# A down projection from seven block products, with its input rows stored by token tile, partition and parity

## Chip, cores, metric

One core of one Trainium2 chip runs the whole program in one launch. The metric is the device time in microseconds; the kernel before has a median of 3306.24 us of 3 runs (3305.8 to 3311.68).

## What is computed

The reference is one decoder block over 16 meta tokens and 2048 tokens of width 1024: two mixing branches (RWKV-7 and S5), their gated sum times `w_out`, and a gated MLP with a causal convolution over tokens. What the change touches most is its end:

```
up = hn @ ffn_w_up                                    # (2064, 1024) @ (1024, 5632)
a  = causal_dwconv(up[..., :2816], conv_w, conv_b)
f  = (gelu_tanh(a) * up[..., 2816:]) @ ffn_w_down     # (2064, 2816) @ (2816, 1024)
h  = h + rms_norm(f, norm_ffn_post)
```

The meta tokens are dropped from the output. All data are float32. Each matrix product is made of three TensorE products: every operand is split into a rounded high part (`_hi`, written by ScalarE as a copy to float32r) and the rest (`_lo`, written by VectorE as raw minus high), and hi*hi, hi*lo and lo*hi are added in PSUM.

## The kernel before

The program is a row of stages, each ended by a barrier of all engines (`stage_ends`): the input projection with the S5 branch, the RWKV chunks (`rwkv_chunks`), the branch mix with the output projection (`branch_mix`, `token_projection` with the name mixout), the up projection (`ffn_up`), and the down projection (`token_projection`, name down). Each engine works through its own list in order and waits on semaphores; nearly all DMAs are issued by SP, in SP's order.

**Down stage.** Two passes over the 22 blocks of 128 hidden channels, 11 blocks (`k_tiles`) in each. In a pass the weights of 11 blocks x 1024 columns are split once, and then 16 token tiles of 128 tokens follow. For each tile, SP loads the hidden values (`load_acts`, 11 blocks x 128 tokens, in runs of 512 bytes since `hidden` is `[22, 128, 2048]` in DRAM), ScalarE makes `a_hi` (L2549), VectorE `a_lo` (L2613), and TensorE runs 11 k x 2 column halves x 3 matmuls (L2516). After pass 0 ScalarE copies PSUM to `sums` (L2555); after pass 1 VectorE adds PSUM to `sums` (L2622), ScalarE squares and takes the root (L2565, L2567), VectorE scales (L2631) and adds the residual rows (L2636), and SP stores the row. The weights of the stage are loaded by L2431 into several spare places; the first is loaded in the up stage (L2840), as is the first input tile (L2843).

**Up stage.** It works already with seven block products in place of eight. It goes over 11 pairs of hidden blocks, first for tokens 0 to 1023 (FIRST), then for 1024 to 2047 (SECOND). In a pair each of 14 parts (q) has its high and low weight made seven parts ahead (L2910, L3030); differences of weights are made by VectorE (L3025). The convolution (L3081, L3083), gelu (L2948) and the gating multiply (`gated`, L3093) follow a half row at a time, and SP stores the half row (L2819). The last half row's gating comes after the last matmul, just before the barrier.

**End of the chunk stage.** Groups of two chunks of 64 tokens are taken one after the other. Behind each group comes a tail: flat copy (L1932), affine on ScalarE (L1938), add and multiply with loaded rows on GpSimd (L2040, L2042), high part on ScalarE (L1942), low part on GpSimd (L2044). SP asks for the mix stage's first weight, activations and gate before that (L1492), and loads the last group's bonus and gate rows (L1433) when the group before it is scaled. The mix stage begins with the split of its first weight (L2223 on ScalarE, L2265 on VectorE), and TensorE's first product there (L2186) waits for it.

## Time and profile before

| | |
|---|---|
| median of 3 runs | 3306.24 us |
| the profiled execution | 3308.43 us, its span 3306.6 us |
| TensorE busy | 3140.9 us, 95% of the span, 25690 matmuls |
| VectorE, ScalarE, GpSimd busy | 1846.0, 1292.4, 120.6 us |
| mean granted TensorE clock | 0.981 |
| last matmuls of the up stage | about 2803 us |
| matmuls of the down stage | 2112, from 2815.7 to 3297.2 us |

All rows below are from this one execution. Times are us from the start of the span unless marked ns. PE is TensorE's matmuls, PEld its weight loads (they run beside the matmuls), DVE is VectorE, ACT is ScalarE, POOL is GpSimd, SPq are SyncE's DMA issues. A line number such as L2516 is that of the kernel above. The granted clock is a share of full speed, 1.00 being 2.4 GHz and 0.50 being 1.2 GHz.

### The profile page before, as it was taken

The page shows a single profiled execution, that of the slowest core. Times are in us where ns is not written, and L with a number is a line of the kernel's source. Part 1 is how long each engine was busy: PE and PEld are TensorE (multiplying, and loading weights), DVE is VectorE, ACT ScalarE, POOL GpSimd, SP SyncE. Part 2 cuts the span into 40 slices and gives each one's busy share as a digit, 9 for nine tenths or more (in the row PEclk, how much of TensorE's full clock was granted, in tenths as well). Part 3 has the DMA queues.
Part 4 walks back from the last instruction along what each step waited for, and adds up shares of the span by engine and source line. Part 5 has one row for each costly group of instructions (what it writes and reads, how often), then busy time and mean ns, then how long its engine had stood idle before and what let it go on. Part 6 is the DMA issues. An engine that isn't in the chain of part 4 may idle for free. (4 is left out here: it accounts for less than half of the span.)

```text
span 3306.6 us, 69209 instructions
## 1 busy us (share of the span) xinstructions
PE 3140.9 (95%) x25690; PEld 2802.9 (85%) x25690; DVE 1846.0 (56%) x3531; ACT 1292.4 (39%) x2265; POOL 120.6 (4%) x126
## 2 busy tenths in 40 slices
PE   8999999999978888879999979999999999999998
PEld 7999989999967777769998869999888887788887
DVE  7666655555545666553344476666766665212333
ACT  6211136767753444441123344444544443312211
POOL 0000000000001222200000000000000000000000
PEclk9999999999988999989999989999999999999999
DMA  5333346656543334333346613333522222412342
GB/s 159 112 138 123 118 156 203 194 188 197 188 122 81 92 92 95 107 121 119 121 160 205 209 57 113 111 102 102 166 83 76 76 82 68 158 51 74 120 125 90
DMA packets 391252, 409.57 MB, mean 124 GB/s; under 512 B 140352, under 2 KB 332736, under 8 KB 387184
## 3 DMA queue, kind: packets, MB, share of 16 engines
q1 hardware_dynamic: 390096, 408.20, 39.5%
q8 instruction: 60, 0.98, 0.1%
q14 instruction: 40, 0.33, 0.0%
q10 hardware_dynamic: 1056, 0.07, 0.0%
HBM read 260.58 MB, written 147.59 MB: 123 GB/s over the span
## 5 line engine op out<-in xcount | busy, mean ns | idle before, releaser
L2889 PE MATMUL psum<-up_x,up_w_hi 128*128 128x512 f32 (+2 forms) x1540 | 353.0, 351 | 12.5 <-ACT up_w_hi L2910 6.9
L2895 PE MATMUL psum<-up_x,up_w_hi 128*128 128x512 f32 (+2 forms) x1540 | 352.8, 351 | 0.8 <-DVE up_x L3047 0.8
L2892 PE MATMUL psum<-up_x,up_w_lo 128*128 128x512 f32 (+2 forms) x1540 | 351.6, 350 | 0.0
L2889 PEld LDWEIGHTS psum<-up_x,up_w_hi 128*128 128x128 f32 x1540 | 260.0, 190 | 54.1 <-issue 7.0
L2895 PEld LDWEIGHTS psum<-up_x,up_w_hi 128*128 128x128 f32 x1540 | 260.0, 190 | 41.3 <-DVE up_x L3047 1.1
L2892 PEld LDWEIGHTS psum<-up_x,up_w_lo 128*128 128x128 f32 x1540 | 260.0, 190 | 40.6
L2516 PE MATMUL psum<-down_w_hi,down_a_hi 128*128 128x512 f32 x704 | 275.0, 391 | 12.3 <-DVE down_w_lo L2675 12.3
L2516 PE MATMUL psum<-down_w_lo,down_a_hi 128*128 128x512 f32 x704 | 274.8, 390 | 0.0
L2516 PE MATMUL psum<-down_w_hi,down_a_lo 128*128 128x512 f32 x704 | 274.8, 390 | 0.0
L694 PE MATMUL psum<-x_hi,proj_w_hi 128*128 128x416 f32 (+1 forms) x640 | 245.5, 384 | 0.0
L577 PE MATMUL psum<-x_hi,proj_w_hi 128*128 128x416 f32 (+1 forms) x640 | 224.7, 351 | 0.0
L694 PE MATMUL psum<-x_lo,proj_w_hi 128*128 128x416 f32 (+1 forms) x640 | 223.8, 350 | 0.0
L577 PE MATMUL psum<-x_hi,proj_w_lo 128*128 128x416 f32 (+1 forms) x640 | 223.4, 349 | 0.0
L577 PE MATMUL psum<-x_lo,proj_w_hi 128*128 128x416 f32 (+1 forms) x640 | 223.4, 349 | 0.0
L694 PE MATMUL psum<-x_hi,proj_w_lo 128*128 128x416 f32 (+1 forms) x640 | 223.3, 349 | 0.0
L3030 DVE TENSOR_TENSOR up_w_lo<-up_weight,up_w_hi 128x512 fp32r<-128x512 f32 x176 | 118.9, 686 | 107.1 <-ACT up_w_hi L2910 107.1
L2516 PEld LDWEIGHTS psum<-down_w_hi,down_a_hi 128*128 128x128 f32 x704 | 132.8, 189 | 40.4 <-issue 12.7
L2613 DVE TENSOR_TENSOR down_a_lo<-down_a_raw,down_a_hi 128x1408 fp32r<-128x1408 f32 x32 | 51.9, 1622 | 196.8 <-ACT down_a_hi L2549 192.8
L2516 PEld LDWEIGHTS psum<-down_w_hi,down_a_lo 128*128 128x128 f32 x704 | 132.7, 188 | 27.7
L2516 PEld LDWEIGHTS psum<-down_w_lo,down_a_hi 128*128 128x128 f32 x704 | 132.7, 189 | 27.6
L2910 ACT ACTIVATE up_w_hi<-up_weight 128x512 fp32r<-128x512 f32 x176 | 109.6, 624 | 85.4 <-PE psum L2895 76.6
L811 ACT ACTIVATE proj_pre<-psum 128x416 f32<-128x416 f32 (+1 forms) x70 | 36.1, 517 | 258.6 <-PE psum L577 203.2
...
## 6 DMA issues: line engine op xcount, KB each, us to landing
...
chunk_pre<-scratch_roles SPq DMA_DIRECT2D x128, 128.0 KB, 2.7
```

What stands on the lines that cost most here:

```text
L577: mm = nc.tensor.matmul(psum[:, PRODUCT_BANKS[n], 0:WIDTHS[n]], w[:, v, k, :], x[:, k, block_of(n)], start=(k == 0 and w is w_hi and x is ...
L694: mm = nc.tensor.matmul(psum[:, GATE_BANKS[n], 0:WIDTHS[n]], w[:, v, k, :], x[:, k, block_of(n)], start=(k == 0 and w is w_hi and x is x_h ...
L811: nc.scalar.activation(pre[:, 2 + STARTS[n]:2 + STARTS[n] + WIDTHS[n]], done, ACT.Copy).then_inc(evacuated, 1)
L2516: mm = nc.tensor.matmul(psum[0:n, 2 * u + h, :], a[:, u, k, 0:n], w[:, k, h * HALF:(h + 1) * HALF], start=(k == 0 and a is a_hi and w is w ...
L2613: nc.vector.tensor_tensor(a_lo[:, u, :, 0:n], (a_raw if n == P else a_meta)[:, :, 0:n], a_hi[:, u, :, 0:n].bitcast(F32), ALU.subtract).the ...
L2889: nc.tensor.matmul(out, w_hi[:, q % 7, k, :], x_hi(phase, step)[:, k, cols], start=opens and k == 0, stop=False, skip_group_check=True)
L2892: nc.tensor.matmul(out, w_lo[:, q % 7, k, :], x_hi(phase, step)[:, k, cols], start=False, stop=False, skip_group_check=True)
L2895: mm = nc.tensor.matmul(out, w_hi[:, q % 7, k, :], x_lo(phase, step)[:, k, cols], start=False, stop=closes and k == K4 - 1, skip_group_che ...
L2910: nc.scalar.activation(w_hi[:, q % 7], weight_of(part, step), ACT.Copy).then_inc(w_hi_ready, 1)
L3030: V.tensor_tensor(w_lo[:, q % 7], weight_of(part, step), w_hi[:, q % 7].bitcast(F32), ALU.subtract).then_inc(w_lo_ready, 1)
```

## The change

The down projection becomes a function of its own, `ffn_down`. Tokens are halved (tile t and tile 8 + t), hidden blocks are halved by parity (block 2k and 2k + 1), output columns are halved (512 and 512). Of the 2 x 2 x 2 block products seven are made, of sums and differences of the quarters, in the order P_2, P_5, P_3, P_1, P_6, P_7, P_4: each of 8 tiles x 11 k x 3 matmuls of 128x512, with one PSUM bank for each tile. The quarters of the result are gathered in `sums`: ScalarE copies them out after P_2, P_5 and P_3, VectorE adds PSUM to them after P_1, P_6 and P_7. The rows of tokens 0 to 1023 are finished after P_6, the others after P_4 straight from PSUM.

The inputs: `hidden` lies in DRAM as `[token tile, partition, parity, 1 + 11, 128]`, with one block of each row unused, so that a tile's input is one run of 5632 bytes per partition; the up stage stores each half row in runs of 512 bytes. In its SECOND phase the up stage also makes the sums S1 = A21 + A22 and S2 = S1 - A11 for each pair (`sum_rows`, two 128x1024 operations on VectorE), loads the A11 row for them and stores both (`hidden_sums`). Two further differences (for P_3 and P_7) are made tile by tile in `ffn_down` (`act_sum`), from two loaded inputs. Weights are handled in items of 128x512, one to four of them in a tile, one product ahead, in a ring of 18; four products need the difference of two loaded weights (`weight_sum`), and two of these differences are stored to DRAM (`w_down_sums`) and loaded again.

At the end of the chunk stage, the last two groups' tail is moved from GpSimd to VectorE, the last group's in two halves by lane; its bonus and gate rows are loaded earlier into `pre`; and the first mix weight is split there (`next_split`) and no longer at the start of the mix stage. For this some buffers get fixed places (`CHUNK_SPACE`).

The diff, cut to its core:

```diff
-    hidden = dram("hidden", [M_FF, P, SEQ])
+    hidden = dram("hidden", [SEQ // P, P, 2, 1 + M_FF // 2, P])
+    hidden_sums = dram("hidden_sums", [2, SEQ // P // 2, P, M_FF // 2, P])
+    w_down_sums = dram("w_down_sums", [2, M_FF // 2, P, D_MODEL // 2])
...
-            for g in (GROUPS - 2, GROUPS - 1):
-                sp.wait_ge(scaled, g)
-                load_post(g)
+            sp.wait_ge(scaled, GROUPS - 2)
+            load_post(GROUPS - 2)
+            sp.wait_ge(toks_done[1], GROUPS)
+            for q_, src in enumerate((gate_dram, bonus_dram)):
+                for lane in BOTH:
+                    at_t = T - WIDE + lane * S
+                    sp.dma_start(pre[:, q_, lane], src[:, :, at_t:at_t + S].rearrange("j p t -> p j t")).then_inc(last_post_loaded, 16)
...
+                    raw, hi, lo, _, hi_made, lo_made = next_split
+                    for n_, part in enumerate((slice(0, 1), slice(1, 3))):
+                        dve.wait_ge(hi_made, n_ + 1)
+                        V.tensor_tensor(lo[:, part], raw[:, part], hi[:, part].bitcast(F32), ALU.subtract).then_inc(lo_made, 1)
                     state(a, 1)
                     for c in (b - 2, a, b):
                         norm_mean(c)
                         norm_squares(c)
                         norm_divide(c)
+                    before = g * WIDE - WIDE
+                    gained(g - 1, 0, flat[:, 1], post[:, 1], post[:, 0], post_loaded, 32 * g)
+                    low_part(g - 1, 0, flat[:, 1], before, WIDE)
+                    for lane in BOTH:
+                        gained(g, lane, flat[:, 0, :, lane * S:(lane + 1) * S], pre[:, 1, lane], pre[:, 0, lane], last_post_loaded, 64)
+                    for lane in BOTH:
+                        low_part(g, lane, flat[:, 0, :, lane * S:(lane + 1) * S], g * WIDE + lane * S, S)
...
+                    raw, hi, _, loaded, hi_made, _ = next_split
+                    act.wait_ge(loaded, 16)
+                    for part in (slice(0, 1), slice(1, 3)):
+                        A.activation(hi[:, part], raw[:, part], ACT.Copy).then_inc(hi_made, 1)
...
-                cols = slice(phase * 2 * UP_COLS, (phase + 1) * 2 * UP_COLS)
-                sp.dma_start(hidden_out[bass.ds(2 * m + half, 1), :, cols].rearrange("m p t -> p (m t)"), hidden[:, half]).then_inc(done, 16)
+                n = 2 * UP_COLS // P
+                sp.dma_start(hidden_out[phase * n:(phase + 1) * n, :, half, bass.ds(m + 1, 1), :].rearrange("t p o c -> p t (o c)"),
+                             hidden[:, half].rearrange("p (t c) -> p t c", c=P)).then_inc(done, 16)
+            def load_row(m):
+                for n in range(2):
+                    sp.wait_ge(rows_stored[n], 16 * m + 16)
+                sp.wait_ge(stored[0], 16 * FF_PAIRS + 16)
+                sp.dma_start(held_a.rearrange("p (t c) -> p t c", c=P),
+                             hidden_out[0:2 * UP_COLS // P, :, 0, bass.ds(m + 1, 1), :].rearrange("t p o c -> p t (o c)")).then_inc(row_loaded, 16)
+            def store_rows(m, done):
+                sp.wait_ge(rows_summed, 2 * m + 2)
+                for n, total in enumerate((held_b, held_a)):
+                    sp.dma_start(hidden_sums[n, :, :, bass.ds(m, 1), :].rearrange("t p o c -> p t (o c)"), total.rearrange("p (t c) -> p t c", c=P)).then_inc(done[n], 16)
...
+                if phase == SECOND and not first:
+                    store_rows(m - 1, rows_stored)
+                if phase == SECOND:
+                    load_row(m)
+                if final:
+                    sp.wait_ge(stored[1], 16 * FF_PAIRS + 16)
+                    sp.wait_ge(product_done[P_1], units_before(SECOND, FF_PAIRS))
+                    sp.wait_ge(product_done[P_2], units_before(SECOND, FF_PAIRS))
+                    sp.dma_start(down_first, down_first_source).then_inc(down_first_loaded, 16)
+                    sp.dma_start(down_w_first, down_w_source).then_inc(down_w_loaded, 16)
...
+            def sum_rows(m, g):
+                dve.wait_ge(b_used[0], g + 2)
+                dve.wait_ge(b_used[1], g + 2)
+                dve.wait_ge(rows_stored[0], 16 * m + 16)
+                V.tensor_tensor(held_b, hidden[:, 0], hidden[:, 1], ALU.add).then_inc(rows_summed, 1)
+                dve.wait_ge(row_loaded, 16 * m + 16)
+                dve.wait_ge(rows_summed, 2 * m + 1)
+                V.tensor_tensor(held_a, held_b, held_a, ALU.subtract).then_inc(rows_summed, 1)
...
+                        if phase == SECOND and not first:
+                            sum_rows(m - 1, g - 1)
...
+            sum_rows(LAST, 2 * FF_PAIRS - 1)
...
+DOWN_RAW, DOWN_W_RAW, DOWN_RING = 4, 4, 18
...
+        ACTS_OF = {P_2: (A12,), P_5: (S1,), P_3: (A12, S2), P_1: (A11,), P_6: (S2,), P_7: (A11, A21), P_4: (A22,)}
...
+        WEIGHTS_OF = {P_2: (B21,), P_5: (B12, B11), P_3: (B22,), P_1: (B11,), P_6: (B22, T1), P_7: (B22, B12), P_4: (B21, T2)}
...
+        def items_in(q):
+            s, t = step_of(q) + 1, tile_of(q)
+            if s == STEPS:
+                return []
+            return [(s, k) for k in range(K_PAIRS) if min(k, TILES - 1) == t]
...
+            def load_act(q, n):
+                j = act_loads.index((q, n))
+                if j >= DOWN_RAW:
+                    sp.wait_ge(acts_lo, act_loads[j - DOWN_RAW][0] + 1)
+                which, t = ACTS_OF[step_of(q)][n], tile_of(q)
+                if which in (S1, S2):
+                    src = act_sums[which - S1, t]
+                else:
+                    src = acts[t + (TILES if which in (A21, A22) else 0), :, 1 if which in (A12, A22) else 0, 1:]
+                sp.dma_start(raw(q, n), src).then_inc(raw_loaded[raw_slot[q, n]], 16)
...
+            def load_weight(s, k):
+                for n, which in enumerate(WEIGHTS_OF[s]):
+                    before = w_loads[w_loads.index((s, k, n)) - DOWN_W_RAW]
+                    sp.wait_ge(w_lo_done, number_of[before[:2]] + 1)
+                    if before[:2] in kept:
+                        kept_stored(before[:2])
+                    if which in (T1, T2):
+                        kept_stored((P_5 if which == T1 else P_6, k))
+                    sp.dma_start(held_w_raw[:, w_slot[s, k, n]], weight_source(which, k)).then_inc(w_raw_loaded[w_slot[s, k, n]], 16)
...
+            def store_kept(s, k):
+                j = kept.index((s, k))
+                sp.wait_ge(w_summed, w_sum_count[s, k])
+                if j >= 2:
+                    kept_stored(kept[j - 2])
+                sp.dma_start(w_sums[0 if s == P_5 else 1, k], held_w_raw[:, w_slot[s, k, 0]]).then_inc(t_stored[j % 2], 16)
...
+            for k in range(DOWN_W_RAW, K_PAIRS):
+                sp.dma_start(weight_raw(0, k), weight_source(B21, k)).then_inc(staged_loaded[k], 16)
+            load_act(1, 0)
+            load_weight(1, 0)
+            load_weight(1, 1)
+            sp.dma_start(gains, gain).then_inc(gain_loaded, 16)
+            for q in range(LAST + 1):
+                if step_of(q) == P_2 and tile_of(q) == TILES - 2:
+                    sp.wait_ge(late_stored, 48)
+                for n in range(len(ACTS_OF[step_of(q + 2)]) if q + 2 <= LAST else 0):
+                    load_act(q + 2, n)
+                for s, k in items_in(q):
+                    if (s, k) in kept:
+                        store_kept(s, k)
+                    if number_of[s, k] + 2 < len(items):
+                        load_weight(*items[number_of[s, k] + 2])
+                if row_of(q) is not None:
+                    load_rows(row_of(q))
+                if q >= 2 and row_of(q - 2) is not None:
+                    store_row(row_of(q - 2))
...
+                opens, closes = s in (P_2, P_5, P_1), s in (P_2, P_3, P_4)
+                if 1 <= s <= 3:
+                    pe.wait_ge(copied, q - TILES + 1)
+                elif s > 3:
+                    pe.wait_ge(added, q - TILES + 1 - 3 * TILES)
+                pe.wait_ge(acts_hi, q + 1)
+                pe.wait_ge(acts_lo, q + 1)
+                for k in range(K_PAIRS):
+                    if t == 0:
+                        pe.wait_ge(w_lo_done, number_of[s, k] + 1)
+                    product(t, q, k, a_hi, w_hi, opens and k == 0, False)
+                    product(t, q, k, a_hi, w_lo, False, False)
+                    mm = product(t, q, k, a_lo, w_hi, False, closes and k == K_PAIRS - 1)
+                    if t == TILES - 1 and k < K_PAIRS - 1:
+                        mm.then_inc(weight_used, 1)
+                mm.then_inc(tile_done, 1)
...
+            high(0)
+            for k in range(6):
+                weight_high(0, k)
+            high(1)
+            for k in range(6, K_PAIRS):
+                weight_high(0, k)
+            nc.scalar.preload_act_table(ACT.Sqrt)
+            act.wait_ge(eps_ready, 1)
+            for q in range(LAST + 1):
+                s = step_of(q)
+                if 1 <= q < LAST:
+                    high(q + 1)
+                if q and step_of(q - 1) in (P_2, P_5, P_3):
+                    copy(q - 1)
+                if s == P_4:
+                    square_known(q)
+                if q and step_of(q - 1) == P_4:
+                    square_second_half(q - 1)
+                for item in items_in(q):
+                    weight_high(*item)
+                if q and step_of(q - 1) == P_6:
+                    square_first_half(q - 1)
+            square_second_half(LAST)
...
+            low(0)
+            for k in range(6):
+                weight_low(0, k)
+            low(1)
+            for k in range(6, K_PAIRS):
+                weight_low(0, k)
+            for q in range(LAST + 1):
+                s = step_of(q)
+                if q and step_of(q - 1) in (P_1, P_6, P_7):
+                    add(q - 1)
+                due = items_in(q)
+                for item in due[:2]:
+                    weight_sum(*item)
+                if 1 <= q < LAST:
+                    low(q + 1)
+                for item in due[:2]:
+                    weight_low(*item)
+                for item in due[2:]:
+                    weight_sum(*item)
+                for item in due[2:]:
+                    weight_low(*item)
+                if q + 2 <= LAST:
+                    act_sum(q + 2)
+                if s == P_4:
+                    if q == TILES * P_4:
+                        dve.wait_ge(gain_loaded, 16)
+                    gain_known(q)
+                if q and step_of(q - 1) == P_6:
+                    if q - 1 == TILES * P_6:
+                        dve.wait_ge(gain_loaded, 16)
+                    finish_first_half(q - 1)
+                if q and step_of(q - 1) == P_4:
+                    finish_second_half(q - 1)
+            finish_second_half(LAST)
```

## Rows read from the trace of the kernel before

**Rows 1.** The chain of waits, in order of time: start, duration, what.

```profile
2815.74 481.47 PE psum L2516 x2112
...
3301.51 1.23 DVE down_sums L2636
```

**Rows 2.** Busy time by stretch; the first row names the columns.

```profile
core 0: us, PE busy (x) PEld busy (x) DVE busy (x) ACT busy (x) POOL busy (x), PEclk, DMA share, GB/s
2600.00:2700.00 100.00, 100.00 (x435) 81.28 (x434) 69.50 (x100) 43.08 (x65) 0.00 (x0) 1.00 0.24 84
2816.00:2818.00 2.00, 2.00 (x5) 1.52 (x5) 1.88 (x2) 1.06 (x1) 0.00 (x0) 0.50 1.02 406
2822.00:2824.00 2.00, 2.00 (x11) 1.65 (x10) 1.94 (x2) 1.72 (x2) 0.00 (x0) 1.00 1.04 418
2860.00:2960.00 100.00, 100.00 (x443) 82.79 (x442) 11.38 (x7) 16.06 (x14) 0.00 (x0) 1.00 0.17 46
```

**Rows 3.** Groups of instructions, 2400 to 3307: busy us, mean ns, idle before.

```profile
L3030 DVE TENSOR_TENSOR up_w_lo<-up_weight,up_w_hi 128x512 fp32r<-128x512 f32 x80 | 54.1, 687 | 50.0 <-ACT up_w_hi L2910 50.0
...
L2613 DVE TENSOR_TENSOR down_a_lo<-down_a_raw,down_a_hi 128x1408 fp32r<-128x1408 f32 x32 | 51.9, 1622 | 196.8 <-ACT down_a_hi L2549 192.8 <-DMA down_gains<-in_ffn_post 4.0
L2910 ACT ACTIVATE up_w_hi<-up_weight 128x512 fp32r<-128x512 f32 x79 | 49.3, 624 | 37.9 <-PE psum L2895 37.9
L2549 ACT ACTIVATE down_a_hi<-down_a_raw 128x1408 fp32r<-128x1408 f32 x32 | 44.0, 1376 | 10.6 <-DMA down_a_raw<-scratch_hidden 6.6 <-PEq L2506 3.3
...
L3067 DVE TENSOR_TENSOR up_a_pre<-psum,up_a_pre 128x512 f32<-128x512 f32 x32 | 22.0, 689 | 12.4 <-PE psum L2895 11.7
...
L2631 DVE SCALAR_TENSOR_TENSOR down_sums<-down_sums,down_stat,down_gains 128x1024 f32 (+1 forms) x16 | 20.6, 1285 | 0.6
L2636 DVE TENSOR_TENSOR down_sums<-down_sums,down_rows 128x1024 f32 (+1 forms) x16 | 19.6, 1226 | 1.3
```

**Rows 4.** DMA queue, 2811 to 2832: packets, MB, share of 16 engines.

```profile
q1 hardware_dynamic: 3334, 7.68, 97.7%
```

**Rows 5.** The DMA queue from 2860 to 2960.

```profile
q1 hardware_dynamic: 9119, 4.62, 16.9%
```

**Rows 6.** The DMA queue from 2748 to 2751.5.

```profile
q1 hardware_dynamic: 288, 0.52, 43.8%
```

**Rows 7.** Timeline from up to down stage: start, duration, engine, instruction, [idle before].

```profile
2808.11 1.23 DVE L3093 TENSOR_TENSOR up_hidden<-up_hidden,up_b_pre 128x1024 f32<-128x1024 f32 x1 [1.12 <-ACT up_hidden L2948]
2811.24 0.06 DVE L2599 MEMSET down_eps<- 128x1 f32 x1 [1.91 <-PEq L3192]
2811.29 0.81 SPq L2431 DMA_DIRECT2D down_w_raw<-in_w_down  x2
...
2812.15 4.04 SPq L2431 DMA_DIRECT2D down_sums<-in_w_down  x8
...
2814.37 1.22 DVE L2675 TENSOR_TENSOR down_w_lo<-down_first_raw,down_w_hi 128x1024 fp32r<-128x1024 f32 x1
...
2815.74 0.76 PE L2516 MATMUL psum<-down_w_hi,down_a_hi 128*128 128x512 f32 x1 [12.26 <-DVE down_w_lo L2675]
```

**Rows 8.** Timeline at the end of the chunk stage.

```profile
1395.47 0.50 SPq L1492 DMA_DIRECT2D mix_weight<-in_w_mix_tiles  x1
...
1407.91 0.38 ACT L1914 ACTIVATE chunk_u<-psum 128x256 f32<-128x256 f32 x1 [5.69 <-PE psum L1530]
...
1409.71 0.42 DVE L1804 TENSOR_TENSOR chunk_m<-chunk_m,psum 128x256 f32<-128x256 f32 x1 [9.19 <-PE psum L1530]
...
1422.49 1.36 DVE L1828 TENSOR_TENSOR chunk_y_unit<-chunk_y,chunk_stat 128x256 f32<-128x256 f32 x1
...
1430.88 1.26 POOL L2044 TENSOR_TENSOR rwkv_y_lo<-chunk_flat,rwkv_y_hi 128x512 fp32r<-128x512 f32 x1 [0.74 <-ACT rwkv_y_hi L1942]
...
1435.41 0.71 PE L2186 MATMUL psum<-rwkv_y_hi,mix_w_hi 128*128 128x416 f32 x1 [10.81 <-ACT mix_w_hi L2223]
```

**Rows 9.** Timeline at the end of the kernel.

```profile
3302.76 0.35 SPq L2423 DMA_DIRECT2D out_h<-down_sums  x1
```

292 lines of the change are left out of this document (254 added, 38 removed).

## The prediction

> **What bounds the kernel now.** I read the chain of waits first. It shows one piece of 481.47 us from 2815.74 on, the 2112 matmuls of L2516 in the down projection, and after it only the few us of the last row [rows 1]. So in this stage TensorE's own work is the time. The stretches say the same: from 2860 to 2960 TensorE is busy all of the time, VectorE 11%, ScalarE 16%, DMA 17%, and the granted clock is 1.00, its level of 2.4 GHz [rows 2]. The pace there is 443 matmuls in 100 us, 0.2257 us each. Over the whole piece it is 481.47 / 2112 = 0.228: at 2816 the clock is at 0.50 (1.2 GHz) after an idle stretch, and at 2822 it is back at 1.00 [rows 2]. The second half of the up stage is bound in the same way, with VectorE at 70% [rows 2].
>
> **Matmuls removed.** Before: 16 token tiles x 22 k blocks x 2 column halves x 3 = 2112. After: 7 block products x 8 tiles x 11 k x 3 = 1848, each of the same shape, three in a row into one bank as before. 264 x 0.2257 = 59.6 us less. (By 0.228 it is 60.2.)
>
> **What the other engines must do beside them.** A tile of a product is now 33 matmuls, 33 x 0.2257 = 7.45 us, where one pass over a tile took twice that. In each, ScalarE makes a_hi (1.38) and 11/8 weight parts (0.62 each); VectorE makes a_lo (1.62) and as many w_lo (0.69) [rows 3]. Added are: the difference of two weights (0.69, as a 128x512 subtract), in tiles of P_3 and P_7 the difference of two inputs (about 1.62, by the a_lo row, same shape), the addition to C out of PSUM (0.69), and for each row of P_6 a scale (1.29) and an add (1.23) [rows 3]. The worst ordinary tile is one of P_6: 0.69 + 0.69 + 1.62 + 0.69 + 0.16 + 1.29 + 1.23 = 6.4 us of 7.45. It fits, if loads are there. The last tile of a product has four weight items instead of one, 3 x 1.38 = 4.1 us more. For the change from P_6 to P_7 this meets the row's 2.7 and the input difference of 1.62: 12.1 us of VectorE in one tile, and in the next again 8.0.
>
> **The stall I expect.** A weight is loaded only two items ahead, so in such a last tile the load of item 9 goes out when w_lo of item 7 is done, some 5 us into the tile, and two loads of 256 KB need 1.5 us of queue (below) and some 2 us of latency. VectorE stands near 3 us there. Then it is at about 16.6 us when it begins the next tile's work, and has a_lo for the tile after ready 3 us later, at 19.6, where TensorE wants it at 14.9: 4.7 us, and 0.5 to 1 in the tile after. I take 5.5 us (bounds 0 and 10). At the other product changes there is neither row nor input difference: VectorE is through at about 11.7, a_lo follows at 14.0 to 14.7, just in time: 0 taken, up to 3 each. A stall may bring the clock down once: the row at 2816 shows the half level after an idle stretch, and the 13 or so matmuls up to 2822 cost about 2.5 us more than at 0.2257. I take 1.5 for this.
>
> **DMA.** The bytes go up from 23 MB of inputs and 11.5 MB of weights to 72 x 0.72 = 52 MB, 121 x 0.262 = 31.7 MB of weights and 5.8 MB of weight differences stored; with rows and results 106 MB in 430 us, 247 GB/s. What the 16 engines do when busy depends on the piece. With nearly all in 4 KB pieces they moved 7.68 MB in 97.7% of 21 us, 374 GB/s [rows 4]; in 512-byte pieces 4.62 MB in 16.9% of 100 us, 273 GB/s [rows 5]; in 2 KB pieces 0.52 MB in 43.8% of 3.5 us, 340 GB/s [rows 6]. The new layout is what makes this bearable: an input tile is read in pieces of 5.6 KB instead of 512 bytes, so 52 MB take 139 us at 374 GB/s and not 190. The worst tiles are those of P_6: 0.72 + 0.72 + 0.52 + 0.52 = 2.5 MB in 7.45 us, 334 GB/s, some 90% of the engines' time. In its last tile it is 1.44 + 2.1 + 1.05 = 4.6 MB, 12 to 13 us of work; the inputs were asked for two tiles ahead, which is why I count this into the 5.5 and not beside it.
> In the Trainium skill, "DMA: Bandwidth & Descriptors", section Specifications, the limit of HBM for one core is put at about 358 GB/s. By that P_6 would run at 93% of the limit and its last tile would take 12.9 us. The trace disagrees on the level: 406 and 418 GB/s in 2 us stretches [rows 2].
>
> **Beginning of the down stage.** The first weight is 512 wide instead of 1024: w_lo takes 0.69 and not 1.22 [rows 3, 7], so TensorE starts 0.5 us sooner. But on ScalarE the split of the second input tile now stands between weights 5 and 6, and its load is behind seven weight loads: these are 1.83 MB and it is 0.72, 6.8 us at 374 GB/s and 2 of latency, 8.8 after the start of the stage. a_hi, w_hi, and on VectorE a_lo and w_lo follow by about 12.3. TensorE, started 3.8 after it and at half clock for some 5 us, wants weight 6 at 10.3. Stall 1.8 us (0 to 4).
>
> **End of the up stage.** It ends with the gating multiply of the last half row (2808.11, 1.23), the barrier, and TensorE's next matmul at 2815.74 [rows 7]. Behind that multiply stand now two sums of 128x1024, 2 x 1.22 by the same row, and two stores that SP can issue only then, 0.4 to 0.5 each by the issues in [rows 7]. Nothing hides them: +3.0 us (2.4 to 4). In the ten pairs before, the same sums (2.4 us of some 38) lie in VectorE's free 30%. The stores in 512-byte pieces and one row load are 2.6 MB, 9.7 us of DMA at 273 GB/s in a pair of 38 us with 24% used. SP holds the sums' stores and waits for them before it fetches a row; the next weights behind them come to land some 5 us before VectorE wants them. Cost 0; up to 1 us per pair if that order bites.
>
> **Chunk stage to mix stage.** Now the last group is finished on GpSimd in three steps of 1.26 one after another with ScalarE between, ending at 1432.14; the mix weights are split after the barrier, and TensorE's wait there is 10.81 [rows 8]. After: the weight split moves to the start of the last group, where ScalarE was idle 5.7 us and VectorE 9.2, and the weight had been asked for at 1395.47 [rows 8]. The tail runs on VectorE in 0.42 to 0.69 steps: previous group added, multiplied (1424.4), high part 1425.1; flat copy and affine of lane 1 on ScalarE until 1426.7; lane 1 add and multiply 1427.6; high 1428.05; two lows, 1428.5. That is 3.6 us sooner; from the end of that work to TensorE it was 3.27, of which about 1.5 were the two splits. 3.6 + 1.5 = 5.1 us saved (3 to 6.5).
>
> **End of the kernel.** After the last matmul (2815.74 + 481.47 = 3297.2) before: add, square, root, reciprocal, scale and add until 3302.74, then the store [rows 1, 9]. After: square of 512 out of PSUM 0.6, gain 0.69, reciprocal 0.17, two halves of 0.66, less than 3 us with handoffs. With the same store behind it: -3.0.
>
> **Sum.** -59.6 + 5.5 + 1.5 - 0.5 + 1.8 + 3.0 - 5.1 - 3.0 = -56.4 us. The profiled execution before took 3308.43 (span 3306.6), so 3252.0; it lay 2.2 above the median of 3306.24, so I predict 3250.
>
> **Rivals.**
> 1. *The weight loads bind at every product change.* If at the other five the round trip (load, difference, high, low) shows too, at 4 us each and with some clock loss: +22, 3272. For it: two items ahead is little, and [rows 6] shows 340 GB/s at best for these pieces. Against: the 7.45 us of slack of the tile after.
> 2. *No stall at all.* If VectorE's backlog is taken up by the two tiles of inputs held: 3250 - 8.8 = 3241. Against: 12.1 + 8.0 us of work stand on VectorE in two tiles of 7.45.
> 3. *The up stage pays.* The sums stand in VectorE's queue ahead of the next pair's weight sums and low parts. At 1 us of TensorE per pair over 11 pairs: 3261. Against: VectorE's free 30%, and low parts made seven steps ahead.
> 4. *Slower: SP's single queue makes each tile a round trip.* All loads, stores and their waits stand in SP's order; the input load of tile q+2 is behind a weight load that waits for w_lo of this tile. If a pair of weights then lands only 5 us after it is asked for and VectorE stands for it in each tile, a tile of P_7 is 5.3 + 5 = 10.3 us, 2.9 too long. The products before a double-weight product have 32 such tiles: 93 us, 3343. It decides from a mean tile of 8.5 us on (56 x 1.05 = 59 us). For it: one queue, and VectorE waiting in order. Against: the load is for the item two further, one whole tile ahead.
> 5. *The change doesn't do what it says* is not left: the loops give 1848.
>
> **Chances.** Forecast 0.55 (own range 3243 to 3260); rival 1 0.17; rival 2 0.12; rival 3 0.08; rival 4 0.08. Between rival 4's full price and the others lies little, so slower by over 0.2% (6.6 us, about what can be told from no change here) gets 0.08, within it 0.02, faster 0.90. Range 3238 to 3280: rival 2 below with the bounds of the start and the tail, rival 1 above.
>
> **What would show it.** L2516's heirs number 1848 at 0.226 us, from first to last about 430 us, with one wait of 4 to 6 us on a_lo or a difference at the start of P_7, and one near 2 us in the first tile. TensorE's wait after the up stage grows from 12.3 to about 15; at the mix stage it falls from 10.8 to 5 or 6. The second half of the up stage keeps 435 matmuls per 100 us. Wrong it is if VectorE waits for weight DMAs in most tiles, if the down stage lasts over 450 us, or if the up stage loses its pace.

## The result, and the profile after

The changed kernel takes 3288.47 us (median of 5 runs, the fastest 3284.51), the kernel before 3309.95 (5 runs). The ratio is 0.9933, with a 95% interval of 0.9919 to 0.9947: 22 us faster, where 56 were forecast, and outside the range of 3238 to 3280. Two of the five runs, at 3500.89 and 13375.18 us, are far off all others and are left out of the ratio. The profiled execution took 3288.47 (span 3286.6, mean clock 0.975).

The chain of waits of the changed kernel shows at once what is different. Where [rows 1] had one piece of 481.47 us there are three pieces of matmuls, and between them weight stores, weight loads and input loads (start, duration, what):

```profile
2841.80 5.05 DMA scratch_w_down_sums<-down_w_raw
2848.28 6.62 DMA scratch_w_down_sums<-down_w_raw
2856.34 6.42 DMA scratch_w_down_sums<-down_w_raw
2864.19 6.50 DMA scratch_w_down_sums<-down_w_raw
2872.12 6.68 DMA scratch_w_down_sums<-down_w_raw
...
2898.94 166.20 PE psum L3402 x726
3066.48 5.75 DMA scratch_w_down_sums<-down_w_raw
3073.19 4.07 DMA scratch_w_down_sums<-down_w_raw
3077.76 3.52 DMA down_w_raw<-scratch_w_down_sums
...
3089.41 31.78 PE psum L3402 x132
...
3127.22 10.33 DMA down_raw<-scratch_hidden
...
3157.27 9.60 DMA down_raw<-scratch_hidden
...
3227.74 52.64 PE psum L3402 x231
```

The stretches, against [rows 2]. The up stage keeps its 435 matmuls in 100 us. 2860 to 2960 holds the border from P_2 to P_5: 413 matmuls and not 443, with a clock of 0.97. The last row is P_6 from its second to its seventh tile:

```profile
core 0: us, PE busy (x) PEld busy (x) DVE busy (x) ACT busy (x) POOL busy (x), PEclk, DMA share, GB/s
2600.00:2700.00 100.00, 100.00 (x435) 81.32 (x434) 74.12 (x102) 43.24 (x66) 0.00 (x0) 1.00 0.38 116
2860.00:2960.00 100.00, 96.45 (x413) 78.85 (x412) 38.86 (x40) 32.07 (x42) 0.00 (x0) 0.97 0.60 201
3090.00:3135.00 45.00, 45.00 (x194) 37.15 (x193) 33.75 (x39) 19.53 (x30) 0.00 (x0) 0.97 0.92 313
```

The timeline from the up to the down stage, against [rows 7], and at the end of the first tile (idle time before an instruction in brackets):

```profile
2805.93 1.22 DVE L3161 TENSOR_TENSOR up_hidden<-up_hidden,up_b_pre 128x1024 f32<-128x1024 f32 x1 [1.12 <-ACT up_hidden L3016]
2807.24 1.23 DVE L3168 TENSOR_TENSOR down_first_raw<-up_hidden 128x1024 f32<-128x1024 f32 x1
2808.57 1.23 DVE L3171 TENSOR_TENSOR down_a_raw<-down_first_raw,down_a_raw 128x1024 f32<-128x1024 f32 x1
...
2812.33 3.97 SPq L3374 DMA_DIRECT2D down_sums<-in_w_down  x7
...
2816.13 1.19 PE L3402 MATMUL psum<-down_w_parts,down_a_hi 128*128 128x512 f32 x2 [14.83 <-DVE down_w_parts L3538]
...
2816.65 0.33 SPq L3335 DMA_DIRECT2D down_raw<-scratch_hidden  x1
...
2823.79 1.38 ACT L3434 ACTIVATE down_a_hi<-down_raw 128x1408 fp32r<-128x1408 f32 x1 [5.92 <-DMA down_raw<-scratch_hidden]
...
2827.48 1.22 PE L3402 MATMUL psum<-down_w_parts,down_a_hi 128*128 128x512 f32 x2 [5.25 <-DVE down_w_parts L3538]
```

TensorE's wait at the mix stage, which was 10.81 [rows 8], and what follows the last matmul of the kernel, where the add of 1.23 stood at 3301.51 [rows 1]:

```profile
1429.09 0.71 PE L2231 MATMUL psum<-rwkv_y_hi,mix_w_hi 128*128 128x416 f32 x1 [6.88 <-DVEq L2301]
...
3279.98 0.39 PE L3402 MATMUL psum<-down_w_parts,down_a_lo 128*128 128x512 f32 x1
3280.41 0.60 ACT L3463 ACTIVATE down_squares<-psum 128x512 bf16<-128x512 f32 x1 [6.41 <-PE psum L3402]
...
3281.95 1.42 DVE L3578 SCALAR_TENSOR_TENSOR down_sums<-down_sums,down_stat,down_rows 128x512 f32<-128x512 f32 x2
3282.73 0.99 SPq L3396 DMA_DIRECT2D out_h<-down_sums  x2
```

**A measure for the rest.** An undisturbed tile of 33 matmuls takes 7.48 us from start to start in this trace, and 44 of the 56 tiles take just that. What a tile takes beyond it I call its loss. In all it is 45.1 us: 10.2 in the first tile, 6.7 at P_2 to P_5, 11.2 at P_1 to P_6, 15.9 at P_6 to P_7, 1.2 at P_7 to P_4. P_3, P_1 and the insides of the products lose nothing. 28 us of it are waits of TensorE. The other 17 are the rest, put down to matmuls at half clock, which the records show at the stage's start and in the stretches that follow the waits. The longest wait at P_1 to P_6 and the longest at P_6 to P_7:

```profile
3082.72 1.22 PE L3402 MATMUL psum<-down_w_parts,down_a_hi 128*128 128x512 f32 x2 [4.00 <-DVE down_w_parts L3538]
...
3161.89 1.19 PE L3402 MATMUL psum<-down_w_parts,down_a_hi 128*128 128x512 f32 x2 [5.10 <-DVE down_a_lo L3518]
```

**What happens at P_1 to P_6.** The timeline of SyncE and VectorE in the last tile of P_1:

```profile
3065.25 0.42 SPq L3335 DMA_DIRECT2D down_raw<-scratch_hidden_sums  x1
3065.76 0.69 DVE L3534 TENSOR_TENSOR down_w_raw<-down_w_raw 128x512 f32<-128x512 f32 x1
3066.48 0.33 SPq L3362 DMA_DIRECT2D scratch_w_down_sums<-down_w_raw  x1
...
3072.30 0.33 SPq L3351 DMA_DIRECT2D down_w_raw<-in_w_down  x1
3072.73 0.37 SPq L3351 DMA_DIRECT2D down_w_raw<-scratch_w_down_sums  x1
3073.19 0.38 SPq L3362 DMA_DIRECT2D scratch_w_down_sums<-down_w_raw  x1
...
3077.32 0.33 SPq L3351 DMA_DIRECT2D down_w_raw<-in_w_down  x1
...
3081.37 0.69 DVE L3534 TENSOR_TENSOR down_w_raw<-down_w_raw 128x512 f32<-128x512 f32 x1 [3.94 <-DMA down_w_raw<-scratch_w_down_sums]
```

Item 7's difference is stored at 3066.48, behind an input of 704 KB, and lands 5.75 later (the chain). Only then may its place be loaded again (3072.30), and only after that does SP come to item 8's store (3073.19), though its difference was ready at 3069.3. This lands 4.07 later, and the next load goes out at 3077.32. So the landing of item 7's store (5.75), that of item 8's (4.07) and the load of item 10 (3.52, from 3077.76) stand one after another: 14.9 us from 3066.48 to the subtraction at 3081.37, while TensorE has one tile of 7.48 us for four items. SP's own waits, 2815 to 3290 (total us, times, longest), show how much of its time goes there:

```profile
SPq L3351 <- DVE down_w_parts L3538: 129.8, 38, 10.7
SPq L3355 <- DMA scratch_w_down_sums<-down_w_raw: 99.8, 22, 6.3
SPq L3335 <- DVE down_a_lo L3518: 55.2, 9, 7.1
```

### The profile page after: what moved, and what is told of

Read it like the earlier page. It is cut to its first block and busy times, and to the rows that moved or that the text cites. A ratio compares the mean times of both kernels' runs of the same rounds, so it can differ in the third digit from the quotient of the medians.

```text
span 3286.6 us, 69045 instructions
## 1 busy us (share of the span) xinstructions
PE 3098.7 (94%) x25426; PEld 2762.6 (84%) x25426; DVE 1985.2 (60%) x3726; ACT 1342.8 (41%) x2373; POOL 114.7 (3%) x120
## 5 line engine op out<-in xcount | busy, mean ns | idle before, releaser
L3402 PE MATMUL psum<-down_w_parts,down_a_hi 128*128 128x512 f32 x1232 | 391.1, 400 | 43.1 <-DVE down_w_parts L3538 29.6
L3402 PEld LDWEIGHTS psum<-down_w_parts,down_a_hi 128*128 128x128 f32 x1232 | 236.6, 193 | 97.8 <-issue 32.1
L3402 PE MATMUL psum<-down_w_parts,down_a_lo 128*128 128x512 f32 x616 | 244.8, 397 | 0.0
L3434 ACT ACTIVATE down_a_hi<-down_raw 128x1408 fp32r<-128x1408 f32 x56 | 77.3, 1380 | 249.0 <-PE psum L3402 187.6
L3518 DVE TENSOR_TENSOR down_a_lo<-down_raw,down_a_hi 128x1408 fp32r<-128x1408 f32 x56 | 91.0, 1625 | 117.3 <-ACT down_a_hi L3434 117.2
L3402 PEld LDWEIGHTS psum<-down_w_parts,down_a_lo 128*128 128x128 f32 x616 | 119.1, 193 | 25.6
L2976 ACT ACTIVATE up_w_hi<-up_t_sums 128x512 fp32r<-128x512 f32 x132 | 82.9, 630 | 138.8 <-PE psum L2961 129.9
```

Source lines behind the costliest of these rows:

```text
L2976: nc.scalar.activation(w_hi[:, q % 7], weight_of(part, step), ACT.Copy).then_inc(w_hi_ready, 1)
L3402: return nc.tensor.matmul(psum[:, bank, :], a[:, q % SLOTS, k, :], w(step_of(q), k), start=opens, stop=closes, skip_group_check=True)
L3434: nc.scalar.activation(a_hi[:, q % SLOTS], raw(q, 0), ACT.Copy).then_inc(acts_hi, 1)
L3518: V.tensor_tensor(a_lo[:, q % SLOTS], raw(q, 0), a_hi[:, q % SLOTS].bitcast(F32), ALU.subtract).then_inc(acts_lo, 1)
```

## The experiments

"Loss" is that of the profiled execution, in the order: first tile, P_2 to P_5, P_1 to P_6, P_6 to P_7, P_7 to P_4. Ratios are to the kernel before, with their 95% intervals; the differences between experiments are of medians. All but e12_chunk_alone change the kernel after. The same code reached the mix stage between 1426.4 and 1435.3 us in these profiles, and the interval of a ratio reaches some 5 us to either side, so differences of less than that between totals aren't told from nothing; they are read from the losses. Nor does a profiled execution always lie at its run's median: e9's is 8.8 us above it, e8's 5.5 below. A border that an edit doesn't touch varies too, P_2 to P_5 between 6.7 and 10.1 us with SP issuing stores and loads as before (after, e4, e5, e10), P_6 to P_7 between 14.2 and 16.5 (after, e1, e2, e3), the first tile between 8.2 and 10.2 (after, e4, e5, e6, e10).

| run | median us | ratio (95%) | loss |
|---|---|---|---|
| after | 3288.5 | 0.9919 to 0.9947 | 10.2, 6.7, 11.2, 15.9, 1.2 = 45.1 |
| e1_no_kept | 3275.1 | 0.9887 to 0.9920 | 9.7, 0, 4.4, 15.7, 2.3 = 32.1 |
| e2_kept_by_act | 3277.0 | 0.9892 to 0.9925 | 9.9, 2.3, 5.6, 14.2, 2.5 = 34.6 |
| e3_act_first | 3286.8 | 0.9912 to 0.9945 | 3.1, 11.2, 10.5, 16.5, 0.6 = 41.9 |
| e4_no_rows_p6 | 3280.7 | 0.9906 to 0.9948 | 8.2, 7.3, 9.1, 10.5, 0.4 = 35.4 |
| e5_no_finish_p6 | 3283.1 | 0.9909 to 0.9942 | 8.2, 9.1, 10.7, 11.2, 2.4 = 41.7 |
| e6_acts_by_act | 3278.6 | 0.9884 to 0.9917 | 8.4, 7.3, 11.2, 11.7, 1.2 = 39.7 |
| e7_old_layout | 3304.0 | 0.9969 to 0.9992 | 11.2, 7.2, 16.2, 24.2, 1.8 = 60.6 |
| e8_order | 3295.3 | 0.9941 to 0.9974 | 8.9, 6.5, 9.4, 21.7, 2.6 = 49.1 |
| e9_five_raw | 3291.8 | 0.9937 to 0.9970 | 7.9, 13.7, 12.8, 17.0, 0 = 51.4 |
| c4_both_by_act | 3273.4 | 0.9883 to 0.9916 | 8.1, 0, 8.5, 12.7, 0.6 = 29.9 |
| e10_p7_one_input | 3283.6 | 0.9913 to 0.9947 | 8.4, 10.1, 9.0, 8.2, 0.1 = 35.8 |
| c8_five_kept_by_act | 3271.6 | 0.9869 to 0.9902 | 7.8, 2.7, 3.5, 15.8, 0 = 29.8 |
| c5_five_by_act | 3262.9 | 0.9847 to 0.9880 | 7.5, 0, 0.8, 10.9, 0 = 19.2 |
| c6_five_act_first | 3256.9 | 0.9823 to 0.9853 | 2.5, 0, 1.8, 9.0, 0 = 13.3 |
| c7_five_first_order | 3262.1 | 0.9844 to 0.9874 | 2.7, 0.8, 1.0, 13.2, 0.5 = 18.1 |
| c9_rows_later | 3254.2 | 0.9824 to 0.9859 | 2.7, 0, 1.7, 7.0, 0 = 11.4 |

**e1_no_kept and e2_kept_by_act.** The stores of weight differences left out (e1: other weights are loaded in their place), or issued by ScalarE instead of SP (e2).

```diff
                 for s, k in items_in(q):
-                    if (s, k) in kept:
-                        store_kept(s, k)
```
```diff
# e2, in ScalarE's weight_high(s, k), after the copy to w_hi
+                if (s, k) in kept:
+                    nc.scalar.dma_start(w_sums[0 if s == P_5 else 1, k], held_w_raw[:, w_slot[s, k, 0]]).then_inc(t_stored[j % 2], 16)
```


> Leaves out the 22 stores of weight differences to DRAM; where such a difference was loaded again, a piece of w_down is loaded in its place, so the P_6 and P_4 products use other weights. In the changed kernel the tiles at the change from P_2 to P_5 lose 6.7 us over 7.48 us each, those at the change from P_1 to P_6 lose 11.2, those around P_6 to P_7 15.9, the first tile 10.2. Theory A (SP stands for each of these stores, whose landing waits behind a 704 KB input load, before it asks for the next weights): P_5's loss falls from 6.7 to below 1, P_6's from 11.2 to below 2; P_7's stays within 2 us; the whole about 16 us faster than the changed kernel, 3272. Rival B (loading only two items ahead is enough by itself to bind when four items fall in one tile): both losses stay above 4 us, the whole at most 6 us faster. Rival C (bytes: the queues are full): these changes gain little, since the stores are 5.8 of some 106 MB; P_7 unchanged.

> Same work as the changed kernel; only the 22 stores of weight differences are issued by ScalarE, right behind its own high part of the same weight, instead of by SP. Theory A (SP's order: the store of item 8 is issued only when SP has passed the load of item 9, which waits for the store of item 7): the chain of 4 to 5 us per item goes, P_5's loss falls from 6.7 to about 1 and P_6's from 11.2 to 2 to 4, 12 to 15 us faster than the changed kernel. If the landing of the stores and not their order is the cause, the losses stay above 5 us each, since SP still waits for the landing before it overwrites the place.

Without the stores 13.4 us go, and with the same stores issued by another engine 11.5 us. So it is not their bytes that cost, but where they are issued. P_2 to P_5 falls from 6.7 to 0 and 2.3, P_1 to P_6 from 11.2 to 4.4 and 5.6. The first tile and P_6 to P_7 stay. In e2 the stores of items 7 to 10 of P_6 are issued at

```profile
3059.40 0.33 ACTq L3447 DMA_DIRECT2D scratch_w_down_sums<-down_w_raw  x1
3060.00 0.33 ACTq L3447 DMA_DIRECT2D scratch_w_down_sums<-down_w_raw  x1
...
3066.65 0.33 ACTq L3447 DMA_DIRECT2D scratch_w_down_sums<-down_w_raw  x1
...
3068.20 0.33 ACTq L3447 DMA_DIRECT2D scratch_w_down_sums<-down_w_raw  x1
```

within 8.8 us, where SP took 17.1 (3066.48, 3073.19, 3078.22, 3083.60). SP still waits for them to land before it loads their places (112.5 us in all, 99.8 in after). The stores also land sooner from ScalarE's queue, 3.7 us in the median against 5.1, and these four in 2.3 to 3.2 against 3.7 to 5.8. How much of the gain is the order of issue and how much the faster landing isn't told apart by these runs. And 4.4 us at P_1 to P_6 aren't the stores' at all, as e1 has none: more than the 2 that theory A left there.

**e3_act_first.** The second input tile is asked for before the seven staged weights.

```diff
+            load_act(1, 0)
             for k in range(DOWN_W_RAW, K_PAIRS):
                 sp.dma_start(weight_raw(0, k), weight_source(B21, k)).then_inc(staged_loaded[k], 16)
-            load_act(1, 0)
```


> One line moved: the load of the second input tile is asked for ahead of the seven staged weight loads and not behind them. In the changed kernel the first tile loses 10.2 us, 5.25 of it a wait in which ScalarE stands for this load (landed 7.1 us after its issue) before it splits weight 6, the rest at half clock. Theory F (the wait is ScalarE's order behind that load): the wait goes to under 1 us and the first tile loses 4 to 6, so 4 to 6 us faster than the changed kernel. Rival (the load's bytes: 2.5 MB at 374 GB/s have to come before weight 6 in any order): the wait shrinks by 1 us at most, since weights 4 to 6 now come behind the 704 KB. All other tiles unchanged.

The first tile's loss falls from 10.2 to 3.1, so its cause is shown. But P_2 to P_5 grows from 6.7 to 11.2, and the median's gain of 1.7 isn't told from nothing. The chain after had a store of 5 to 6.7 us in each tile of P_2, so SP may lag there already and lose behind what is won ahead; that is argued, not shown. The same edit on c5, where P_2 to P_5 loses nothing, is c6, and there it holds.

**e4_no_rows_p6, e5_no_finish_p6.** What the rows of tokens 0 to 1023 add in P_6: e4 leaves out the loads of rows 2 to 7 and the stores of rows 0 to 7, e5 the scaling and the full residual add of these rows on VectorE.

```diff
# e4
-                if row_of(q) is not None:
+                if row_of(q) is not None and (row_of(q) < 2 or row_of(q) >= TILES):
                     load_rows(row_of(q))
```
```diff
# e5
-                V.scalar_tensor_tensor(total, total, stat[:, r, 4:5], gains, ALU.mult, ALU.mult).then_inc(scaled, 1)
...
-                V.tensor_tensor(total, total, rows[r % 2], ALU.add).then_inc(finished, 1)
+                V.tensor_tensor(total[:, 0:1], total[:, 0:1], rows[r % 2][:, 0:1], ALU.add).then_inc(finished, 1)
```


> Leaves out the residual loads of token rows 2 to 7 and the stores of result rows 0 to 7, which in the changed kernel go beside P_6 (some 7 MB in 60 us); VectorE's work is the same. Theory D (the loss of 15.9 us around P_7 comes from DMA queues that are full in P_6, so that the two inputs per tile of P_7 land 8 to 10 us after they are asked for): the loss falls to 5 us or less, landing of these inputs to about 6 us. Rival E (VectorE's 12 and 8 us of work in the two tiles): the loss stays above 11. P_5 and P_6 keep 6.7 and 9 to 11.

> Leaves out, for token rows 0 to 7, the scale by the norm and the full add of the residual (2.5 us of VectorE per tile of P_6); all DMAs stay. Rival E (VectorE's load): the loss around P_7 falls from 15.9 to below 8. Theory D (full queues): it stays above 11. P_5 and P_6 unchanged.

Each takes about 5 us off P_6 to P_7 (15.9 to 10.5 and 11.2). Neither alone is the cause. In e4 the inputs that took 10.33 and 9.60 us to land take 6.7 and 8.2, and still two thirds of the loss stay; in e5 they take 10.0 and 10.3.

**e6_acts_by_act.** The input loads of tiles 2 to 55 are issued by ScalarE, at the start of a tile, so they no longer stand behind SP's waits.

```diff
# ScalarE
             for q in range(LAST + 1):
+                for n in range(len(ACTS_OF[step_of(q + 2)]) if q + 2 <= LAST else 0):
+                    load_act(act, nc.scalar, q + 2, n)
```


> Same work as the changed kernel; the input loads of tiles 2 to 55 are issued by ScalarE at the beginning of each tile, on its own DMA queue, instead of by SP. Theory D2 (the inputs of P_7 are late because SP reaches them late and weights stand behind them in one queue): the loss around P_7 falls from 15.9 to below 10, P_6 and P_5 by 2 to 3 us each, since the weight stores no longer wait behind 704 KB; 6 to 12 us faster. If full queues are the cause, the loss around P_7 stays above 13 and the whole is within 4 us of the changed kernel.

9.9 us of the median, but 5.4 of the losses: 4.2 at P_6 to P_7, short of the 6 expected, and 1.8 in the first tile, which the edit doesn't touch and which varies by as much. P_2 to P_5 and P_1 to P_6 gain nothing, where 2 to 3 us each were expected. The rest of the 9.9 isn't the edit's: e6's profile begins the down stage at 2812.0 and after's at 2816.1, and nothing was changed before that.

**e7_old_layout.** The rearranged hidden rows and sums undone, all else kept.

```diff
-    hidden = dram("hidden", [SEQ // P, P, 2, 1 + M_FF // 2, P])
-    hidden_sums = dram("hidden_sums", [2, SEQ // P // 2, P, M_FF // 2, P])
+    hidden = dram("hidden", [M_FF, P, SEQ])
+    hidden_sums = dram("hidden_sums", [2, M_FF // 2, P, SEQ // 2])
```


> Undoes the layout alone: the hidden values and their sums lie as before, by block, partition and token, so that half rows are stored in runs of 4 KB and a tile's input is loaded in 1408 runs of 512 bytes instead of 128 of 5632. By the rows before, 704 KB in 512-byte pieces take 2.6 us of the engines and 1.9 in long ones: 72 loads, 53 us more DMA time in a stage of 464. Theory G (the layout matters where the queues are full): P_7 and the tiles of P_7 with two inputs lose 10 to 20 us more than 15.9, P_6 2 to 4 more; the whole 12 to 30 us slower than the changed kernel, 3300 to 3318. Rival (hidden by prefetch): within 4 us of 3288.

15.6 us slower than after: without the layout the whole change brings 0.2% (ratio 0.9981), and most of that is the chunk stage's (e12, 0.1%). The last six tiles of P_6, e7 first and then after, show why: the short pieces fill the DMA engines' time (101% by the profile's account) and bring 304 GB/s, where after moves 313 in 90% (348 when busy); and an input takes 7.7 us from issue to landing in the median, after 6.5.

```profile
3106.60:3154.20 47.60, 45.08 (x200) 37.06 (x198) 36.58 (x42) 18.91 (x28) 0.00 (x0) 1.00 1.01 304
```
```profile
3098.60:3145.50 46.90, 45.02 (x199) 36.98 (x198) 36.95 (x43) 18.91 (x28) 0.00 (x0) 1.00 0.90 313
```

**e8_order.** VectorE makes the low part of the next input before the weight differences, and the input difference and the finished row before items 9 and 10.

```diff
                 due = items_in(q)
-                for item in due[:2]:
-                    weight_sum(*item)
                 if 1 <= q < LAST:
                     low(q + 1)
+                for item in due[:2]:
+                    weight_sum(*item)
...
+                # after act_sum and finish_first_half
+                for item in due[2:]:
+                    weight_sum(*item)
```


> Same work, another order on VectorE and ScalarE: in each tile a_lo of the next tile comes before the weight differences instead of behind them, and the input difference and the finishing of a row come before weight items 9 and 10 instead of behind. Theory H (VectorE's order: what TensorE needs next stands behind a difference that waits for a weight load): the loss around P_7 falls from 15.9 to below 9, P_6's from 11.2 by 3 to 5, P_5's to 3 to 6; 8 to 14 us faster. Rival (the loads themselves are late): gain below 4 us, the waits only change their name.

P_6 to P_7 grows to 21.7. My theory that VectorE merely did things in a bad order has fallen. VectorE's two waits for weight loads there shrink (3.75 and 1.82 us to 0.59 and 0.80), but what is moved ahead waits for a late input: at 3165.69 VectorE stands 7.35 us for `down_raw<-scratch_hidden`, where after has 4.63.

**e9_five_raw.** A fifth place for raw weights, and each load issued as soon as its place is free, not two items ahead.

```diff
-DOWN_RAW, DOWN_W_RAW, DOWN_RING = 4, 4, 18
+DOWN_RAW, DOWN_W_RAW, DOWN_RING = 4, 5, 18
...
-                    if number_of[s, k] + 2 < len(items):
-                        load_weight(*items[number_of[s, k] + 2])
+                    load_weights_after((s, k))
```


> Five places for raw down weights instead of four, and each load issued as soon as its place is free instead of two items ahead. Theory A (what is left of the loss at the borders of the products is the round trip of a weight that is asked for too late: wait for w_lo, store, load): the loads lie one half to two items further ahead, and of the 45.1 us that the down stage's 56 tiles lose over 7.48 us each, 6 to 12 go, at P_2 to P_5, P_1 to P_6 and P_6 to P_7: 3276 to 3282 us. Theory B (VectorE's own work and the input loads set it): within 2 us of 3288.

Theory A is out: no gain, 3.3 us slower than after with overlapping intervals, and P_2 to P_5 loses 13.7. SP's waits for the stores grow from 99.8 to 110.5 us, and those for a place to be used (on VectorE's w_lo) from 129.8 to 184.3. In its timeline a load of a place, the other load and the next store still follow one another in SP's list, 4 to 6 us apart:

```profile
3084.53 0.38 SPq L3354 DMA_DIRECT2D down_w_raw<-in_w_down  x1
3085.00 0.38 SPq L3365 DMA_DIRECT2D scratch_w_down_sums<-down_w_raw  x1
3090.59 0.32 SPq L3354 DMA_DIRECT2D down_w_raw<-scratch_w_down_sums  x1
3091.00 0.38 SPq L3354 DMA_DIRECT2D down_w_raw<-in_w_down  x1
3091.47 0.38 SPq L3365 DMA_DIRECT2D scratch_w_down_sums<-down_w_raw  x1
```

**c4_both_by_act, c8_five_kept_by_act, c5_five_by_act.** c4 is e2 and e6 together; c8 is e2 and e9; c5 is all three.

> The stores of weight differences and the input loads of tiles 2 to 55 are both issued by ScalarE. Alone the one gave 3277.0 and the other 3278.6 against 3288.5. If the two take away the same wait (SP's single order): 3274 to 3278. If they are separate, they add up: 3267 to 3271.

> Five places and the stores of weight differences by ScalarE, all input loads by SP. If the stores in SP's order were what made five places useless there (3291.8): about 3266 to 3272. If input loads behind waiting weight loads count as much: 3275 to 3280, with the P_5 and P_6 borders still losing 5 us or more.

> Both issues by ScalarE and five raw weight places. Theory A: 4 to 8 us better than the run without the fifth place, 3262 to 3272. Theory B: the same as that run within 2 us.

c4 gains 15.1 us by the medians, where its two edits alone gained 11.5 and 9.9; by the losses it is 15.2 against 10.5 and 5.4, nearly their sum, so that they take away the same wait isn't shown. It keeps 8.5 us at P_1 to P_6, more than e2 alone. With the stores out of SP's list the fifth place, useless before, is worth 5.4 us (e2 to c8), and with the inputs out too 10.5 (c4 to c5). Seen the other way, moving the stores is worth 20.2 us beside five places (e9 to c8) and 11.5 beside four. The input loads add 8.7 (c8 to c5). P_2 to P_5 and P_1 to P_6 are down to 0 and 0.8: that was SP's order and the depth of the loads together.

**e10_p7_one_input.** P_7 takes one input instead of the difference of two.

```diff
-P_7: (A11, A21), P_4: (A22,)}
+P_7: (A11,), P_4: (A22,)}
```


> P_7 takes one input tile instead of the difference of two: 8 loads of 0.72 MB and 8 subtractions of 1.6 us are left out. If the two inputs of 0.72 MB, asked for in the full queue at the end of P_6, are what starves P_7's first tiles: the loss at P_6 to P_7 falls from 15.9 us to 4 to 6, time 3276 to 3280. If the weights' round trip sets it: it falls by no more than 3 us, 3285 to 3288.

P_6 to P_7 falls from 15.9 to 8.2, by half and not to the 4 to 6 expected, where e4 and e5 took a third each. Inputs, rows and weights crowd the DMA engines and VectorE together there, and every burden taken away gives some 5 to 8 us. The three sum to 17.8 of 15.9, so they overlap, and no run splits the loss between DMA and VectorE.

**e12_chunk_alone.** The kernel before with the change at the end of the chunk stage alone.

> The kernel before with the change at the end of the chunk stage alone (tail on VectorE, rows loaded earlier, first mix weight split there). The sum had 5.1 us for it (3 to 6.5); the waits in the profile after fit with about 4 to 6. If that holds: 5 us faster than before, 3303 to 3305 beside a before of 3309. If the tail's work on VectorE slows the last group elsewhere: within 2 us of before.

3306.86 against 3310.59 us, ratio 0.9988 (0.9979 to 0.9997): by the ratio 4.0 us, between 1.0 and 7.0. TensorE's wait there is the one of the kernel after:

```profile
1428.19 0.71 PE L2231 MATMUL psum<-rwkv_y_hi,mix_w_hi 128*128 128x416 f32 x1 [6.87 <-DVEq L2301]
```

**c6_five_act_first, c7_five_first_order, c9_rows_later.** c6 is c5 with e3's edit, c7 is c6 with e8's. c9 is c6 with the last two rows of P_6 finished and stored three tiles later:

```diff
-                if q and step_of(q - 1) == P_6:
+                done = q - 1 if q < TILES * P_7 - 1 else q - 4
+                if q and step_of(done) == P_6 and (q < TILES * P_7 - 1 or tile_of(done) >= TILES - 2):
```


> As the run with both issues by ScalarE and five places (3262.9), and the second input tile is asked for before the staged weights. If the stall in the first tile is this load's place in the queue: the first tile's loss falls from 7.6 to about 2.6 us (what the half clock at the stage's start costs), 3257 to 3260. If the staged weights are only made late instead: unchanged, 3261 to 3265, with the wait on a weight in the same tile.

> As the run before it, and VectorE makes the low part of the next input first in a tile, and the input difference and the finished row before the weight items 9 and 10, whose loads come late. If order around the late load makes the loss at P_6 to P_7: that loss falls from 10.9 to 4 to 7 us, total 3252 to 3256. If VectorE has no idle time there to fill: within 2 us of the run without the order change, 3256 to 3260. Alone, with four places and SP issuing all, this order made things slower (3295), so a loss of 5 us is the third case.

> As c6, and the scaling and the residual add of rows 6 and 7 (2.7 us of VectorE each) stand in tiles 2 and 3 of P_7 in place of the last tile of P_6 and the first of P_7, with their stores behind them. If VectorE's backlog in these two tiles makes the loss at P_6 to P_7: it falls from 9.0 us by 4 to 6, and the median from 3256.9 to 3251 to 3254. If the late loads of items 9 and 10 and of the inputs make it: it falls by less than 2 us, 3255 to 3258.

c6 takes 3256.9 us, 1.6% under before (0.9838, 0.9823 to 0.9853): the first tile's loss is 2.5, what the half clock costs there. The order change makes it worse again (c7, 13.2 at P_6 to P_7). c9 takes 2.0 off P_6 to P_7, and its 3254.2 (3247.2 to 3261.9) isn't told from c6. TensorE's two waits at P_7, in c6 and then in c9:

```profile
3132.97 1.19 PE L3391 MATMUL psum<-down_w_parts,down_a_hi 128*128 128x512 f32 x2 [5.32 <-DVE down_a_lo L3516]
3143.90 0.70 PE L3391 MATMUL psum<-down_w_parts,down_a_hi 128*128 128x512 f32 x2 [1.09 <-DVE down_a_lo L3516]
```
```profile
3129.91 1.00 PE L3393 MATMUL psum<-down_w_parts,down_a_hi 128*128 128x512 f32 x2 [2.92 <-DVE down_a_lo L3518]
3141.18 0.70 PE L3393 MATMUL psum<-down_w_parts,down_a_hi 128*128 128x512 f32 x2 [1.91 <-DVE down_a_lo L3518]
```

The first wait shrinks by 2.4 when 2.7 us of work leave the tile, so that much looks like VectorE's backlog; before it VectorE also stands 3.8 us for two weight loads (c6). The second grows by 0.8: in both chains a `down_raw<-scratch_hidden` stands before it, 10.02 us in c6 and 10.36 in c9. These inputs land in a stretch where DMA is full (c6, 3130 to 3137: 99%, 376 GB/s), and c6's was asked for only at 3126.6, 6.6 us after P_7 had begun, when ScalarE had come to it in its own list. One profile of each gives these 2.0 us, and the border varies by 2.3 where it isn't touched, so the split stays open. How far an earlier issue of the inputs would help wasn't tried.

## Why the prediction was wrong

By its own terms, forecast and measured, in us:

| term | forecast | measured | from |
|---|---|---|---|
| 264 matmuls | -59.6 | -59.8 | 264 x 7.48 / 33 |
| first tile | +1.8 | +7.6 | 10.2, less the 2.6 that before lost in its first tile (17.54 for 14.96) |
| P_2 to P_5 | 0 | +6.7 | losses |
| P_1 to P_6 | 0 | +11.2 | losses |
| P_6 to P_7, with the clock | +7.0 | +15.9 | losses |
| P_7 to P_4 | 0 | +1.2 | losses |
| end of up stage, start of down | +2.5 | +2.6 | 14.83 - 12.26 |
| chunk to mix | -5.1 | -4.0 | e12 |
| end of the kernel | -3.0 | -3.2 | 9.4 to 6.2 from the last matmul to the end of the span |
| sum | -56.4 | -21.8 | the medians: -21.5 |

**The step that failed** is "At the other product changes there is neither row nor input difference: VectorE is through at about 11.7, a_lo follows at 14.0 to 14.7, just in time: 0 taken, up to 3 each". It is 17.9 of the 34.6 us missing (6.7 and 11.2). It counted VectorE's work and one load, but not that the weight differences of P_5 and P_6 are stored before their place may be loaded, and that SP issues nothing else while it waits: [rows 6] priced a DMA's transfer, and a store's landing time of 5.1 us in the median (2.0 to 6.7) was in no term. Without the stores 4.4 of the 17.9 are left (e1), with the stores on ScalarE's list 7.9 (e2); what e1 leaves can't be the stores', and c5 shows that with the order and the depth mended the two borders cost 0.8 us together. Rival 1 named the place (3272, at 0.17) with a load's round trip and not the store's.

**P_6 to P_7** had the right mechanism and half its size: 7.0 against 15.9. I had DMA at 12 to 13 us for the last tile and counted it "into the 5.5 and not beside it"; but the inputs of P_7 land 10.33 and 9.60 us after their issue, and VectorE, in order, does nothing behind the difference that waits for them. VectorE's backlog and the full DMA both have a part (e4, e5, e10 lose 5.4, 4.7 and 7.7 us less); how the loss splits between them stays open. The forecast's 2.5 MB for an ordinary tile of P_6 is a slip: 0.72 + 0.52 + 0.52 + 0.52 are 2.3, which is what 313 GB/s give in 7.48 us.

**The first tile** had the right place and a wrong end: 8.8 us from the start of the stage to the landing was forecast. The second input landed 2823.79 - 2812.33 = 11.5 us after it, as SP took 3.97 us to issue the seven loads before it and the landing took 7.12 from its own issue. That made a wait of 5.25 us where 1.8 was forecast. The half clock, which came again after the wait, is the rest; the 10.2 are also the most that any profile with this order shows but e7's.

**Right** were the count and price of the matmuls, the pace of the up stage (875.9 us from its first to its last matmul, and 875.8 in e12, which has no sums in it, so rival 3 is out), the two sums and stores behind its last gating, the tail, and the chunk stage within its interval. Rival 4, SP's single queue, was priced as a cost of every tile and given 0.08; the trace shows nothing of it inside the products; what there is of it stands at their borders. The Trainium skill, "Trainium Kernel Development and Optimization", section Key Constraints, says that issuing DMAs from several engines only saves the sequencer's issue time. For 22 stores of 0.38 us that would be 8.4 us at most, and SP, which waits for over 300 us in this stage, is short of no issue time. The runs disagree with "only": moving these 22 stores to ScalarE's list took 20.2 us off beside five places (e9 to c8). In this kernel a wait in SP's list held up the stores behind it (17.1 us for four, 8.8 from ScalarE), and the stores landed sooner as well (6.0 us in the median in e9, 4.6 in c8).

The forecast of 3250 is nearly what the kernel does once the issue lists, the depth and the first tile's order are mended: 3256.9 (c6), and 432.0 us from first to last matmul of the down stage where about 430 was written.
